# Rotary products of the dilated heads: from VectorE to GpSimd, shuffle and sum stay

## The reference

```python
def _partial_rope(x, positions):
    half = ROPE_DIM // 2
    ...
    x1 = xf[..., :half]
    x2 = xf[..., half:ROPE_DIM]
    out = jnp.concatenate([x1 * cos - x2 * sin, x2 * cos + x1 * sin, xf[..., ROPE_DIM:]], axis=-1)
```

## Time and profile before

| what | value |
|---|---|
| median of three runs | 1572.83 us |
| profiled execution | 1572.4 us, span 1570.5 us |
| TensorE, VectorE, ScalarE, GpSimd busy | 96%, 70%, 51%, 1% |
| TensorE's granted clock over the span | 0.995 |
| attention of the dilated units | from about 71 to 341 us of the span |

### The profile page before, as it was taken

One profiled execution on the slowest core, in us unless ns is written; L12 is line 12 of the kernel. 1 busy time (PEld: TensorE's weight loads), 2 busy tenths in 40 slices (PEclk: granted clock), 3 DMA queues, 4 the chain that ended last, 5 costly groups with the idle time before them and its releaser, 6 DMA issues. The chain is left out here.

```text
span 1570.5 us, 20831 instructions
## 1 busy us (share of the span) xinstructions
PE 1509.0 (96%) x7364; PEld 1243.4 (79%) x7364; DVE 1092.4 (70%) x1747; ACT 795.7 (51%) x1438; POOL 9.5 (1%) x24
## 2 busy tenths in 40 slices
PE   6999999999999999999999999999999899999997
PEld 5788888876888887788888878888888677777776
DVE  4687777656666768743665676666666887777776
ACT  5577666654777775434134543343334444444442
POOL 1000000000000000000000000000000000000001
PEclk9999999999999999999999999999999999999999
DMA  5211111110121113333645424444446664444402
GB/s 188 95 59 37 41 57 38 41 36 19 40 56 55 28 42 99 90 118 118 210 124 141 135 87 152 164 151 151 148 148 206 243 228 148 147 148 148 148 27 108
DMA packets 168277, 173.40 MB, mean 110 GB/s; under 512 B 7848, under 2 KB 127720, under 8 KB 167792
## 3 DMA queue, kind: packets, MB, share of 16 engines
q1 hardware_dynamic: 168176, 172.07, 33.9%
HBM read 125.84 MB, written 46.20 MB: 110 GB/s over the span
## 5 line engine op out<-in xcount | busy, mean ns | idle before, releaser
L1141 PE MATMUL ps<-hspl,wsp 128*128 128x512 f32 x1536 | 422.0, 407 | 7.3 <-DVE wsp L2110 3.2
L1141 PEld LDWEIGHTS ps<-hspl,wsp 128*128 128x128 f32 x1536 | 265.0, 189 | 53.7 <-issue 6.7
L1498 PE MATMUL ps<-dn_b,a_hi 128*128 128x512 f32 x896 | 279.0, 393 | 17.2 <-DVE keep L2342 11.4
L1498 PEld LDWEIGHTS ps<-dn_b,a_hi 128*128 128x128 f32 x896 | 167.3, 189 | 59.6 <-issue 21.8
L1498 PE MATMUL ps<-dn_b,a_lo 128*128 128x512 f32 x448 | 175.2, 391 | 0.0
L2342 DVE TENSOR_TENSOR keep<-keep,ps 128x512 f32<-128x512 f32 (+1 forms) x144 | 101.5, 713 | 42.3 <-PE ps L1498 23.9
L1498 PE MATMUL ps<-up_b,a_hi 128*128 128x512 f32 x384 | 118.4, 390 | 0.4 <-DVE up_b L2342 0.4
L1958 ACT ACTIVATE keep<-keep 128x512 f32<-128x512 f32 x64 | 40.5, 633 | 125.5 <-DVE keep L2644 42.0
L1498 PEld LDWEIGHTS ps<-dn_b,a_lo 128*128 128x128 f32 x448 | 84.4, 188 | 17.8
L2342 DVE TENSOR_TENSOR dn_b<-dn_raw,dn_b 128x1024 fp32r<-128x1024 f32 x56 | 67.1, 1221 | 39.7 <-ACT dn_b L1974 39.7
L2229 DVE TENSOR_TENSOR keep<-ps,o_part 64x256 f32<-64x256 f32 x80 | 39.7, 496 | 71.7 <-ACT o_part L1679 71.0
(11 more groups left out here) (242 smaller groups left out, 2819.8 us busy)
## 6 DMA issues: line engine op xcount, KB each, us to landing
hidden<-keep SPq DMA_DIRECT2D x112, 256.0 KB, 2.2
dn_raw<-hidden SPq DMA_DIRECT2D x56, 512.0 KB, 6.0
raw<-in_w_in SPq DMA_DIRECT2D x35, 512.0 KB, 3.8
a_raw<-in_w_up SPq DMA_DIRECT2D x36, 256.0 KB, 3.1
sgl<-sg SPq DMA_DIRECT2D x8, 1024.0 KB, 5.1
a_raw<-in_w_down SPq DMA_DIRECT2D x32, 256.0 KB, 3.1
spare<-in_w_down SPq DMA_DIRECT2D x32, 256.0 KB, 4.1
spare<-in_w_up SPq DMA_DIRECT2D x28, 256.0 KB, 3.2
```

What stands on the lines that cost most here:

```text
L1141: ins = pe.matmul(psp(u, g), wsp[c % 2][:, wp, k * P:(k + 1) * P], hspl[:, mp, k, cols], start=(n == 0), stop=(n == 23), skip_group_check= ...
L1498: ins = pe.matmul(o, a_part(n, j, wp, k), b_block(n, j, mp, k), start=(first and k == 0 and m == 0), stop=(k == ks - 1 and m == 2), skip_g ...
```

## The change

For the units after the first, the two products of each half go to GpSimd, which works through them in a loop of its own: for each unit, for keys and then queries, for each half, it waits until the shuffle is done (`roped`), multiplies the half by the cosine and the scratch by the sine, and counts `pool_mul` up by two. VectorE keeps the shuffle and the sum, which now waits for `pool_mul`. `roped` counts 4 for keys or queries of a unit in place of 8, and `rotated(u, n)` gives the new counts to those who wait. The table of jobs has 8 entries: the shuffles stay in steps 3, 6, 9 and 12, and the sums are in steps 5, 7, 11 and 13. Unit 0 is rotated on VectorE as before. The semaphore of the last two products, `y_pool`, is now a later count of `pool_mul`.

```diff
-ROTATE_OPS = {3: (0,), 4: (1,), 5: (2, 3), 6: (4, 5), 7: (6, 7), 9: (8,), 10: (9,), 11: (10, 11),
-              12: (12, 13), 13: (14, 15)}
+ROTATE_OPS = {3: (0,), 5: (1,), 6: (2,), 7: (3,), 9: (4,), 11: (5,), 12: (6,), 13: (7,)}
+
+def rotated(u, n):
+    return 8 * n if u == 0 else 8 + 8 * u + 4 * n
...
                 if t in (2, 4) and j == 2:
-                    sp.wait_ge(roped, 16 * t)
+                    sp.wait_ge(roped, rotated(t - 1, 2))
...
+            for u in range(1, N_DIL):
+                pool.wait_ge(table_in, 16 * (u // 2 + 1))
+                for which in range(2):
+                    for half in range(2):
+                        x = group_half((k_raw, q_raw(u))[which], u, half)
+                        other = group_half(v_raw, u, half)
+                        cos, sin = group_half(rope_c, u, half), group_half(rope_s, u, half)
+                        pool.wait_ge(roped, rotated(u, which) + 2 * half + 1)
+                        pool.tensor_tensor(x, x, cos, ALU.mult).then_inc(pool_mul, 1)
+                        pool.tensor_tensor(other, other, sin, ALU.mult).then_inc(pool_mul, 1)
+
             pool.wait_ge(table_in, 16 * (len(DILATIONS) + 1))
...
-                        act.wait_ge(roped, 16 * u + 16)
+                        act.wait_ge(roped, rotated(u, 2))
...
-                else:
-                    dve.wait_ge(roped, 16 * u + 8 * which + 4 * half + n)
+                elif u:
+                    dve.wait_ge(pool_mul, 8 * (u - 1) + 4 * which + 2 * half + 2)
+                    ins = dve.tensor_tensor(x, x, other, ALU.add)
+                else:
+                    dve.wait_ge(roped, 8 * which + 4 * half + n)
...
-                    jobs += [lambda n=n: rotate(u, n // 8, n // 4 % 2, n % 4) for n in ROTATE_OPS.get(s, ())]
+                    jobs += [lambda n=n: rotate(u, n // 4, n // 2 % 2, n % 2) for n in ROTATE_OPS.get(s, ())]
```

More of the change, by code:

```diff
@@ L626, in build @@
         y_scaled = sem("y_scaled")
-        y_pool = sem("y_pool")
+        pool_mul = sem("pool_mul")
         lexp_ok = sem("lexp_ok")
@@ L1012, in _ @@
                 if n in Y_POOL:
-                    sp.wait_ge(y_pool, Y_POOL.index(n) + 1)
+                    sp.wait_ge(pool_mul, 8 * (N_DIL - 1) + Y_POOL.index(n) + 1)
                 else:
@@ L1064, in _ @@
                 pool.wait_ge(y_scaled, k + 1)
-                pool.tensor_tensor(y_tile[Y_ORDER[n]], y_tile[Y_ORDER[n]], f_g[:], ALU.mult).then_inc(y_pool, 1)
+                pool.tensor_tensor(y_tile[Y_ORDER[n]], y_tile[Y_ORDER[n]], f_g[:], ALU.mult).then_inc(pool_mul, 1)
         N_CONST = 7 + 2 + 6 + 1 + 2
@@ L1623, in k_stack @@
                 if u < N_DIL:
-                    act.wait_ge(roped, 16 * u + 8)
+                    act.wait_ge(roped, rotated(u, 1))
                 after(act, qk_done, STEPS * (u - 1))
@@ L1634, in query_hi @@
                     if t < N_DIL:
-                        act.wait_ge(roped, 16 * t + 16)
+                        act.wait_ge(roped, rotated(t, 2))
                     after(act, qk_done, 2 * B - 2)
```

## The result

The changed kernel took 1578.03 us (median of 19 runs, 1573.51 to 1582.52), the kernel before 1573.64 in the same series (19 runs, 1570.71 to 1576.29). The ratio is 1.0024, with a 95% interval of 1.0015 to 1.0033: slower by 3.8 us, between 2.4 and 5.2 (the ratio is not that of the two medians, which differ by 4.4). The mean granted clock was 0.9936 in the runs of the changed kernel and 0.9935 in 29 other runs of the kernel before, so the clock is not what differs. The time is inside the forecast range (1571.5 to 1579.0), but only because the range was stretched to reach over the first rival: the forecast's own case, 1573.3 us with a range of 1571.8 to 1575.5, is not what happened. What happened is the first rival: VectorE's instructions with two operands in SBUF stand still beside GpSimd's products.

The account below looks back on a forecast made before the run. TensorE was taken to set the pace. At most 0.7 us gained counted as nothing and 0.5 us lost at the waiting adds gave 1573.3 us for the median, against 1572.83 before; range 1571.5 to 1579.0.

Parts of the forecast that it names:

- the first rival: VectorE's two-operand instructions block behind GpSimd's products: about 1.0 us a unit, 5.0 in all, 1577.8 us; chance 0.34.
- the forecast's own case: Blocking absent or partial, GpSimd products near 1.3 us: 0.5 us lost, 1573.3 us for the median; chance 0.52.
- What bounds the stretch: 70 to 300 us: TensorE sets the pace; relieving VectorE of two products per half gains at most about 0.7 us.
- rival 3: VectorE's relief reaches TensorE: 0.26 us a unit, 1.3 us gained, 1571.5 us; chance 0.05.
- The product's duration: A GpSimd product of 128 x 512 takes 1.27 us, between 1.18 and 2.36.
- Rival 2: GpSimd's product takes much longer than half: 1578.6 us at 1.8 us each, 1584 at 2.36; chance 0.09.
- The new wait: VectorE's add waits for GpSimd's pair, some 1.7 us in step 7; about 0.5 us lost over five units.
- What GpSimd's reads do to VectorE: Instructions beside GpSimd's products: by the nearest row no slowing, by the other end up to 1.27 us each.
- Rival 1: Blocking in the keys' pairs: step 5's maxes 1.0 us late, costing 0.4; then the output sum 0.5 to 0.6 late.
- the second pair: Keys' second half, shuffle in step 6, add in step 7: under blocking, the output sum comes 0.5 to 0.6 us late.
- The queries' pairs: Steps 9 to 13: VectorE saves two products and the output sums wait for ScalarE anyway, so nothing is later.

Follow-up runs that it names:

- the hand-over alone: The changed kernel with each pair of GpSimd products replaced by four fills that read nothing, the add still waiting: 1570.44 us against 1573.70 of the kernel before.

## Why the prediction was right and wrong

- *What bounds the stretch* held: TensorE sets the pace, and relief of VectorE is worth little. With the hand-over alone the units gained 0.9 us, a little over the "at most about 0.7", where the sum counted nothing. So the relief of rival 3 exists, smaller than its 1.3 us, but in the change itself the blocking outweighs it.
- *The product's duration* held: 1.27 us forecast from two rows, 1.28 to 1.30 measured where nothing is beside it, rows cut in 4 or 16 runs too (192.76 and 283.46 us: 1.28 each). Rival 2 falls; the longer products are those that waited for VectorE.
- *The new wait* was forecast at 1.7 us in step 7 and came out at 0.78, because the low part's wait ate the rest; in the fifth unit at 2.16. Without the reads, behind the shorter fills, step 7 showed 1.34 to 1.62. As a cost by itself the wait was put at 0.5 us; the fills show a gain of 0.9, and some 0.4 of loss, by the estimate above, had they been as long as the products.
- *What GpSimd's reads do to VectorE* is the step that failed: "By the row nearest, no slowing". The sum put this term at nothing; it is nearly all of the 4.03 us. The nearest row was an instruction with one operand in PSUM, and the ones in question have two in SBUF. Nearness in the trace was taken for likeness, where the number of SBUF operands is what decides. The Trainium skill's page "SBUF — State Buffer" (section "Who interferes with whom") separates just these two kinds. This case's rows agree with it on both: 0.68 and 0.40 us became 1.42 and 1.43 beside a product, 425 ns of the maxes stayed 426, and fills that read nothing left 415 at 415. The section also says that the order of issue decides who stands still. The rows bear that out at 89.08 us, where the product had started first, but not by their starts at 177.15, where the product that had started 0.49 us earlier stood. The rule was in the text as a rival with 0.34; by what it says of these operands it should have been the forecast.
- *Rival 1's size.* 1.0 us a unit and 5.0 in all, measured 0.94, 0.97, 0.66, 0.56, 0.90 and 4.03. In the first unit the maxes of step 5 were put 1.0 us late and came 0.76 late; the second pair "0.5 to 0.6", measured 1.19 - 0.78 = 0.41. In the third to fifth unit the split was not blocked (0.68 and 0.69), there GpSimd waited. The queries' pairs were rightly left at nothing.
- *Chances.* No change within 0.2% had 0.58, slower 0.38; the ratio 1.0024 lies just beyond the bound, its interval on both sides of it. That the time lies in the range is owed to the rival and not to the forecast's mechanism.

## What to carry to other kernels

Before an element-wise operation goes from VectorE to GpSimd, list the instructions that VectorE runs during its time and count those with two operands in SBUF: in this kernel each of them and a GpSimd product that reads SBUF took turns, a whole instruction at a time. If there is room, place the pair where VectorE works from PSUM; the same 40 products cost 3.8 us beside such instructions, and a step further on nothing that the runs tell from zero (ratio 1.0002, 0.96 us in the units). And check that the wait at the taker is shorter than the work it was rid of.

## What was not expected of the hardware

- A tenth of a microsecond can change which engine pays, and the earlier start does not always win. A 0.40 us instruction of VectorE became 1.43 us behind a product that had 0.14 us of lead, and stayed 0.40 when both started at 274.48, where the product became 1.56. Yet a lead of 0.49 us did not keep the product of 176.66 from standing; why is open.
- Fills on GpSimd (128 x 512, 0.57 us each) did not slow VectorE (the low part 415 ns as before): it is the reading.
- Where VectorE kept its own products beside GpSimd's, the loss in the units was 11.6 us: VectorE's products were blocked too (994 ns in place of 687), so that in the changed kernel, where these two products are gone from VectorE, part of what GpSimd's reads cost doesn't show. That this makes the whole difference to the 4.03 us is argued, not tested.
